# Rotary half-swap by SBUF-to-SBUF copies in place of permutation products

## What is computed

```
def apply_rope(x, cos, sin):
    half = x.shape[-1] // 2
    ...
    x1, x2 = x[..., :half], x[..., half:]
    return jnp.concatenate([x1 * c - x2 * s, x2 * c + x1 * s], axis=-1)
...
qa = apply_rope(rms_norm(qa.reshape(B, S, A_HEADS, HEAD_DIM), qn_a[i]), cos64, sin64)
```

## Time and profile before

| | us |
|---|---|
| median of three runs | 2590.4 |
| lowest and highest run | 2590.0, 2590.89 |
| span of the profiled execution | 2589.5 |
| PE busy in it | 2536.0 (98%) |
| DVE busy | 1838.2 (71%) |
| ACT busy | 1304.3 (50%) |
| POOL busy | 116.2 (4%) |

### The profile page before, as it was taken

How to read it: one execution, slowest core, us unless ns; L and a number is a source line. 1 busy time by engine, 2 the same in 40 slices (tenths; PEclk the granted TensorE clock), 3 DMA queues, 4 the chain that set the end, 5 groups by cost and what they waited for, 6 DMA issues and landing times.

```text
span 2589.5 us, 41592 instructions
## 1 busy us (share of the span) xinstructions
PE 2536.0 (98%) x16522; PEld 2192.0 (85%) x16522; DVE 1838.2 (71%) x2257; ACT 1304.3 (50%) x1535; POOL 116.2 (4%) x125
## 2 busy tenths in 40 slices
PE   8999999999999999999999999999999999999997
PEld 7888999888999988789989887788888888888886
DVE  6647767855777565375554843698898888988988
ACT  5554545453544421234334212377677677777765
POOL 1100000300000011100000110000000000000000
PEclk9999999999999999999999999899999999999998
DMA  5344553423555331136544212489989999999995
GB/s 213 140 183 159 183 181 145 144 97 134 212 180 195 131 131 66 66 147 235 182 151 164 106 66 98 171 332 357 353 339 354 344 347 358 348 349 344 352 353 211
DMA packets 77326, 558.21 MB, mean 216 GB/s; under 512 B 8704, under 2 KB 8960, under 8 KB 9856
## 3 DMA queue, kind: packets, MB, share of 16 engines
q1 hardware_dynamic: 76320, 550.93, 57.4%
q0 software_dynamic: 864, 5.24, 0.5%
HBM read 555.09 MB, written 1.05 MB: 215 GB/s over the span
## 4 chain that ended last, share of the span: by engine, by line
PE 91%; DVE 4%; ACT 2%; issue 2%; DMA 0%; DVEq 0%; ACTq 0%; SPq 0%; POOL 0%
PE bank L648 23%; PE bank L1137 18%; PE bank L1162 10%; PE bank L638 9%; PE bank L677 7%; PE bank L709 4%; PE bank L729 3%; PE bank L662 2%; PE bank L1110 1%; DVE w_lo L2489 1%; PE bank L1147 1%; PE bank L956 1%; PE bank L970 1%; PE bank L967 1%; ACT w_hi L1645 1%
## 5 line engine op out<-in xcount | busy, mean ns | idle before, releaser
L2489 DVE TENSOR_TENSOR w_lo<-ring,w_hi 128x2048 fp32r<-128x2048 f32 x216 | 486.2, 2288 | 54.1 <-ACT w_hi L1645 53.0
L1645 ACT ACTIVATE w_hi<-ring 128x2048 fp32r<-128x2048 f32 x216 | 404.9, 1916 | 20.6 <-PE bank L1137 17.0
L1137 PE MATMUL bank<-w_hi,xe_hi 128*128 128x512 f32 x792 | 311.4, 393 | 1.1
L1137 PE MATMUL bank<-w_hi,xe_lo 128*128 128x512 f32 x792 | 308.7, 390 | 0.0
L1137 PE MATMUL bank<-w_lo,xe_hi 128*128 128x512 f32 x792 | 308.5, 390 | 0.0
L648 PE MATMUL bank<-x_hi,w_hi 128*128 128x256 f32 x1008 | 285.3, 283 | 0.0
L648 PE MATMUL bank<-x_hi,w_lo 128*128 128x256 f32 x1008 | 285.2, 283 | 0.0
L648 PE MATMUL bank<-x_lo,w_hi 128*128 128x256 f32 x1008 | 285.2, 283 | 0.0
L1740 DVE TENSOR_TENSOR w_lo<-ring,w_hi 128x2048 fp32r<-128x2048 f32 x97 | 222.1, 2290 | 86.5 <-ACT w_hi L1266 84.4
L638 PE MATMUL bank<-xT,ring 128*128 128x256 f32 x1088 | 253.8, 385 | 1.1 <-ACT Z L1554 1.1
L1266 ACT ACTIVATE w_hi<-ring 128x2048 fp32r<-128x2048 f32 x99 | 189.4, 1913 | 109.4 <-PE bank L677 71.4
(11 more groups left out here) (371 smaller groups left out, 5127.4 us busy)
## 6 DMA issues: line engine op xcount, KB each, us to landing
ring<-in_stream SPq DMA_DIRECT2D x431, 1024.0 KB, 5.1
yT<-in_stream SPq DMA_DIRECT2D x54, 1024.0 KB, 6.9
xT<-in_stream SPq DMA_DIRECT2D x27, 1024.0 KB, 7.1
Z<-in_stream SPq DMA_DIRECT2D x8, 1024.0 KB, 8.1
norm_rows<-in_rows POOLq DMA_DIRECT2D x4, 1024.0 KB, 8.5
par<-in_par SPq DMA_DIRECT2D x1, 1335.0 KB, 9.6
cst<-in_cst SPq DMA_DIRECT2D x1, 1216.0 KB, 13.3
xres<-in_x SPq DMA_DIRECT2D x2, 512.0 KB, 4.1
```

The source lines that it names most:

```text
L1137: r = mm(banks[4 + j % 2], a[:, k, :], moe_part(b, i)[:, q * 512:(q + 1) * 512], start=(k == 0 and a is xe_hi and b is w_hi), stop=(k == K ...
L1645: act_(moe_part(w_hi, at), moe_slot(at), ACT.Copy).then_inc(*A.done("moe_hi", at))
L2489: v.tensor_tensor(moe_part(w_lo, at), moe_slot(at), moe_part(w_hi, at).bitcast(F32), ALU.subtract)\
```

## The change

The permutation products go, and with them the matrices `rot64` and `rot32` in the constants (256 of their columns). In their place SP, in the same queue as the weights, copies the halves of each pair from `qk` to `rot` with their places exchanged: the rows of a half go to the rows of the other. That is four copies of 32 partitions for pairs 0 to 4, and eight of 16 partitions for pairs 5 and 6, each 512 columns wide (256 for pair 4). They are issued after the load of the unit that is six further than the pair's own (`SWAP_AFTER`), once the pair's gains are done and, from pair 2 on, once the pair that used the same half of `rot` has been added. The negative sign of the first half moves into the table of sines. DVE's sine product works in place on `rot`, and it and GpSimd's cosine product, which overwrites `qk`, now wait for the copies (`halves_swapped`).

```
         PAIR_UNIT = [0, 1, 3, 4, 5, 6, 7]
+        SWAP_AFTER = 6
+
+        def half_rows(i):
+
+            half = 32 if QK_PAIRS[i][0] < 9 else 16
+            return [(slice(a, a + half), slice(a ^ half, (a ^ half) + half)) for a in range(0, P, half)]
+
+        def halves_swapped(l, i):
+
+            per = [len(half_rows(n)) for n in range(len(QK_PAIRS))]
+            return s_halves, 16 * (l * sum(per) + sum(per[:i + 1]))
...
+            def swap_halves(l, i):
+
+                c, m = QK_PAIRS[i]
+                sp.wait_ge(*V.of("qn", l, i))
+                if i >= 2:
+                    sp.wait_ge(*G.of("roped", l, i - 2))
+                for to, of in half_rows(i):
+                    sp.dma_start(rot[to, i % 2, 0:m * SEQ], qk[of, c * SEQ:(c + m) * SEQ]).then_inc(s_halves, 16)
...
                 sp.dma_start(slot(u), stream[u]).then_inc(s_slot[HOME[u]], 16)
+                if u < MIX2_0 and u % LAYER1 - SWAP_AFTER in PAIR_UNIT:
+                    swap_halves(u // LAYER1, PAIR_UNIT.index(u % LAYER1 - SWAP_AFTER))
...
-                    elif kind == "rotate":
-                        rotate(l, n)
...
-            def rotate(l, i):
-                c, m = QK_PAIRS[i]
-                pe.wait_ge(*V.of("qn", l, i))
-                if i >= 1:
-                    pe.wait_ge(*V.of("rotsin", l, i - 1))
-                mm(banks[7][:, 0:m * SEQ], ct("rot64" if c < 9 else "rot32"), qk[:, c * SEQ:(c + m) * SEQ],
-                   start=True, stop=True).then_inc(*T.done("rotated", l, i))
...
-                    ve.wait_ge(*T.of("rotated", l, i))
-                    if i >= 2:
-                        ve.wait_ge(*G.of("roped", l, i - 2))
-                    v.tensor_tensor(halves(rot[:, i % 2, 0:w]), halves(banks[7][:, 0:w]),
+                    ve.wait_ge(*halves_swapped(l, i))
+                    v.tensor_tensor(halves(rot[:, i % 2, 0:w]), halves(rot[:, i % 2, 0:w]),
...
-                    po.wait_ge(*T.of("rotated", l, i))
+                    po.wait_ge(*halves_swapped(l, i))
...
-            c[f"sin{dim}"] = np.sin(ang).astype(f)
+            c[f"sin{dim}"] = sign * np.sin(ang).astype(f)
```

More of the change, by code:

```diff
@@ L146, in const_names @@
     n = Names()
-    for name, w in (("ident", 128), ("ones64", 128), ("ones32", 128), ("rot64", 128), ("rot32", 128), ("mean256", 128),
+    for name, w in (("ident", 128), ("ones64", 128), ("ones32", 128), ("mean256", 128),
                     ("causal", 384), ("window", 384), ("cos64", 256), ("sin64", 256), ("cos32", 256), ("sin32", 256),
@@ L304, in emit @@
         s_out = ctx.enter_context(nc.semaphore("out_stored"))
+        s_halves = ctx.enter_context(nc.semaphore("halves_swapped"))
         s_slot = [ctx.enter_context(nc.semaphore(f"slot{i}_loaded")) for i in range(RING + 2)]
@@ L2665, in constants @@
         half = dim // 2
[L2666 to L2672, removed]
+        sign = np.where(np.arange(P) % dim < half, -1.0, 1.0).astype(f)[:, None]
         inv = (f(1.0) / np.power(f(10000.0), np.arange(0, dim, 2, dtype=f) / f(dim))).astype(f)
```

## The result

The changed kernel takes 2612.8 us (median of four runs, 2611.2 to 2614.7), the kernel before 2590.6 in the same comparison: a ratio of 1.0084, with a 95% interval of 1.0072 to 1.0097. The profiled execution has a span of 2612.8 us and belongs to the longest of the four runs, 2614.65. The forecast was 2596.1 us with a range up to 2606: the sign is right, the size is four times too small.

A forecast was written before the change was run, and what follows sets the result against it. It took PE and DVE as matched within 0.2 us in the input units, so copy waits make pair 6's gains 2.2 us late per layer: 4.4 + 1.3 for the clock = 5.7 us, giving 2596.1 us, range 2589 to 2606.

The forecast's parts named there:

- What bounds the stretch: Input units of each layer: PE has no gap, DVE little room; 7.2 us a pair against 7.4 a PE unit.
- D: Time from the end of a pair's gains to its last copy's landing: 3.2 us for four copies, 5.1 for eight.
- The signs of it: DVE idle before sine products (0.9, 2.8 us), PE idle 1.3 before unit 5 and about 4 before the third score.
- What goes: Seven permutation products on PE, 5.6 us, and a 0.61 us wait: 6.2 us a layer, 12.4 if nothing replaces them.
- the row of the store: Profile row of a 512 KB store from SBUF: 2.6 us to landing, 1.2 without its movement; used to bound a copy's landing.
- L: A copy's landing counted from its issue: taken as 1.7 us, between 1.4 and 2.6; 10 us of total per us.
- The clock: PE's waits before the third score and transposes: one low-clock stretch a layer, one more than before, costing 1.3 us.
- The sum of the forecast: Pair-by-pair ends of the gains in layer 0: pair 6 at 87.5 us in place of 85.31, 2.2 us later.
- GpSimd: Its cosine product starts 1 to 4 us later, at a cost of nothing.
- The slow one: Rival: copies queue behind the weight load and land at 2.6 us; pair 6 6.7 us late, 2605.1 us; chance 0.18.
- The hidden one: Rival: copies hide behind DVE's low part if D is 2.3 or less; pair 6 at about 82, 2583.7 us; chance 0.10.

The follow-up runs named there:

- before_waits: Kernel before, products kept, plus 72 copies between halves of a spare buffer, with DVE waiting for their landing before each sine product: 2617.5 us, ratio 1.0102.
- copies_first: Changed kernel with each pair's copies issued ahead of the weight load they stood behind (SWAP_AFTER 5 in place of 6): 2612.6 us, ratio 1.0082.
- light_gpsimd: Changed kernel with GpSimd's cosine product and addition over 8 columns in place of 512 or 256: 2608.2 us, ratio 1.0065.
- one_copy: Changed kernel with one copy of all 128 rows per pair in place of four or eight, leaving out the exchange of halves: 2588.98 us, ratio 0.9989.
- sine_later: Changed kernel with DVE's sine product one unit later in its order and two semaphores in turn for the copies: 2588.11 us, ratio 0.9985.
- eight_copies: Changed kernel with eight copies of 16 rows for every pair (pairs 0 to 4 had four of 32): 2636.35 us, ratio 1.0175.

## Why the forecast was right in sign and wrong in size

**What bounds the stretch: right.** The forecast said that DVE and PE are matched within 0.2 us, so that a wait in DVE's queue passes on. It does: the wait alone gave 26 us, and 1.7 to 2.5 us more of D in each of pairs 0 to 4 gave 23.5. The signs of it that the forecast named came, all larger: DVE waited 3.00, 1.66 and 4.14 us for pairs 0, 1 and 5 (0.9, 0.9 and 2.8 forecast), PE 3.55 us for unit 5 (1.3) and 6.52 for a score (4).

**What goes: right, and worth little here.** PE lost 5.6 us of products a layer, and with them 1.5 us came off the path to pair 2's gains (before_waits against the changed kernel), where the forecast had 1.0. Busy time was to fall by 9 to 12 us; it rose from 2536.0 to 2537.6, and PE's idle time rose by 21.7 us. Products at 1.2 GHz last longer (0.41 us a record where it is 0.28 at full clock), which fits the rise; no run separates it.

**D: the step that failed.** Its form was right (issues in a row, then a landing of fixed length), both terms were too small:

- The spacing of the issues was taken from loads, 0.47; these copies go out 0.63 apart. One copy of 128 rows alone was issued in 0.47, so it isn't the kind of transfer; whether it is the number of rows, the exchange or the row of copies behind one another isn't shown. Four copies: 0.37 us more. Eight: 1.0 more.
- The landing was taken at 1.7, between 1.4 and 2.6, and is 2.0 (1.8 at least). The forecast drew it toward the row of the store, 1.2 fixed plus movement. The rule of the Trainium skill, page "SBUF — State Buffer", section "The DMA setup-cost knee (why "@ 1 MiB" ≠ asymptote)" (some 2 us per DMA whatever its size), which the forecast had put aside, is nearer: the estimate from it was 2.15. The trace agrees with it within 0.15 us.
- A load in front, for which 0.3 us were allowed in L for all pairs, adds nothing to most and 1.0 us to pair 2 of layer 0 (copies_first took it away). Pair 0 of layer 0 and pair 3 of layer 1 landed 1.3 and 1.6 us late for a reason that no run shows.

That gives 3.87 and 6.35 as the floor, where the forecast had 3.2 and 5.1. By the measured rows pair for pair, D was above the forecast by 2.0 (pair 0), 1.7 (pair 2), 0.7 (pair 3), 1.3 (pair 4, one of its issues took 1.36) and 1.25 (pair 5): 6.9 us of layer 0. Pair 1's 0.7 doesn't count, as pair 2 hangs on unit 5. In layer 1 the same pairs make 5.3. So D, the mis-sized term, is 12.2 of the 17.6 us by which the profiled span (23.3 longer) went past the forecast (5.7).

**The clock: right that it would, wrong where and how often.** The forecast had one stretch a layer, behind the scores. There was another behind PE's 3.55 us wait in unit 5: 1.6 us on the path to pair 2's gains. The forecast also put the start of unit 5 before the change at 47.64, from the chain, where its first product starts at 47.47: 0.2 more. The sum of the forecast, 87.5, with 6.9 of D, these 1.8 and 0.6 for pair 4's slowed gains is 96.8; 96.45 was measured. Behind pair 6, layer 0 loses a further 3.7 us (14.8 - 11.1) where 1.3 were allowed: the last sine product is 1.1 longer, and 24 products after the transposes take 4.6 us in place of 3.03. Layer 1 adds 8.5 us, less than layer 0: its D for pair 0 is 3.86, not 5.2, and the kernel before had a low stretch of its own there.

**GpSimd: wrong.** "Starts 1 to 4 us later: nothing" asked only who waits for it, not what runs beside it. In the changed kernel its work came to lie beside the low part of unit 6, the gains of pair 4 and the last sine product; light_gpsimd prices that at 4.6 us. The forecast also let the sine product keep its 0.68 us with both operands in SBUF; alone it does (0.69), beside GpSimd's product it took 1.78.

**The rivals.** The slow one named a landing behind the weight load at 2.6 us for every pair, and gave 2605. The time went beyond it, but by its mechanism in one pair only (pair 2 of layer 0): with the load out of the way the runs stayed where they were. The mean D of pairs 0 to 4 in layer 0, 4.5 us, is above the 4.1 that it would have given, by the issues and by pair 0. The hidden one was refuted as put (D of 2.3 or less), yet one_copy, with 2.37, shows that its condition was the right one, and its 82 us for pair 6 is what sine_later reached (81.7). It forecast 2583.7 for that case; 2588 was measured, since part of the gain goes to the low clock behind the transposes, which it had left out.

**Open:** why pair 0 in layer 0 lands 1.3 us late, with its copies behind the load or before it, and pair 0 in layer 1 doesn't; why pair 3 of layer 1 lands late in one execution and not in another; and what in the changed kernel makes up for GpSimd's 4.6 us.

## What to carry to other kernels

Before a product is replaced by a transfer, count the transfers that the layout forces, not the bytes: here each of them held the queue for 0.63 us and the last one landed 2.0 us later, which is 3.9 us for what PE did in 0.86. Such a latency did no harm here when the engine that consumes it had other work queued in front of the wait: the same 72 copies cost 22 us directly behind the gains and nothing one unit later. And move the consumer first, then ask what the freed engine gives, which is only the distance to the next bound: here 3 us of 12.4, if anything.

## What the runs showed of the hardware

- An issue from SP's queue took 0.47 us for one copy of 128 rows and 0.59 (0.63 from start to start) for copies of 32 or 16 rows in a row, 0.51 for the first of most groups, single ones up to 1.4 (1.7 in eight_copies). The landing took 1.8 us at least, 2.0 in the median, for 64 KB and for 32 KB alike, and 3.6 at most.
- A copy of 256 KB in one piece landed in 1.9 us at least, 2.3 in the median and 4.7 at most (one_copy), so four of 64 KB cost more mainly by their issues.
- Single operations of DVE beside a GpSimd operation on 512 columns took longer: 3.37 in place of 2.29 us (2048 columns, beside product and addition), 1.09 in place of 0.48 (256, beside an addition) and 1.78 in place of 0.69 (512, beside a product that had begun before it). They were back at their length when GpSimd's work was 8 columns wide. The addition on GpSimd was slowed as well: 3.22 in place of 1.29 us at 51.96. The slowed one ended about its own usual duration behind the end of the other. Not all are slowed: the reciprocal at 41.92, with one operand and beside GpSimd's product and addition, took its 3.35 us, and sine products that read a bank kept 0.68.
- PE's waits of 2.66 and 3.55 us were each followed by stretches at the 1.2 GHz level (0.58, 0.50 and 0.51 granted in windows of 3 us), its waits of 1.43 and 1.25 us were not. Over the span the mean clock fell from 0.992 to 0.986.
